# A mixer and mixture-of-experts layer on one core: row-tiled scatter, larger weight transfers, a reordered router and four experts written out

## What is computed

```
h      = rms_norm(x, norm_ffn_g)
logits = h @ w_router + b_router               # 256 x 32
top_v, top_e = top_k(logits, 4);  gate = softmax(top_v)
for each expert e, on the rows that chose it:
    gu = h @ w_gate_up[e] + b_gate_up[e]       # 1024 -> 2048
    g, lin = min(gu[:1024], 7), clip(gu[1024:], -7, 7)
    act = g * sigmoid(1.702 * g) * (lin + 1)
    y   = act @ w_down[e] + b_down[e]          # 1024 -> 1024
x = x + sum of gate * y over the four experts of a token
out = rms_norm(x, norm_final_g)
```

## Time and profile before

| | |
|---|---|
| median of 3 runs | 1145.58 us (1144.92 to 1145.92) |
| profiled execution | 1142.67 us, its span 1140.9 us |
| TensorE busy | 1113.5 us, 98% of the span |
| DVE, ACT, POOL busy | 24%, 16%, 7% |
| mean granted clock of TensorE | 0.988 |
| moved by transfers | 431.89 MB, 379 GB/s over the span |

### The profile page before, as it was taken

One profiled execution on the slowest core, in us unless ns is written; L12 is line 12 of the kernel. 1 busy time (PEld: TensorE's weight loads), 2 busy tenths in 40 slices (PEclk: granted clock), 3 DMA queues, 4 the chain that ended last, 5 costly groups with the idle time before them and its releaser, 6 DMA issues.

```text
span 1140.9 us, 12748 instructions
## 1 busy us (share of the span) xinstructions
PE 1113.5 (98%) x4959; PEld 490.8 (43%) x4960; DVE 273.7 (24%) x661; ACT 179.5 (16%) x333; POOL 75.9 (7%) x155
## 2 busy tenths in 40 slices
PE   7999899899999999999999999999999999999997
PEld 6888685533333333333333333333333333333332
DVE  3999761311111111111111111111111111111112
ACT  3011221111111111111111111111111111111112
POOL 2975100000000000000000000000000000000000
PEclk9999899799999999999999999999999999999999
DMA  8843479489999999999999999999999999999994
GB/s 225 268 157 139 159 304 374 185 327 410 418 418 428 430 427 429 429 427 430 427 429 429 429 429 429 427 430 427 428 429 427 430 427 428 429 429 429 429 427 191
DMA packets 51618, 431.89 MB, mean 379 GB/s; under 512 B 6465, under 2 KB 22255, under 8 KB 25390
## 3 DMA queue, kind: packets, MB, share of 16 engines
q1 hardware_dynamic: 51598, 431.62, 91.2%
HBM read 430.56 MB, written 1.05 MB: 378 GB/s over the span
## 4 chain that ended last, share of the span: by engine, by line
PE 89%; DVE 9%; issue 1%; ACT 1%; DMA 0%; DVEq 0%; another core or an unknown queue 0%; SPq 0%; POOL 0%; POOLq 0%
PE bank L1286 39%; PE bank L1298 20%; PE bank L1306 10%; DVE bank L814 6%; PE bank L1259 5%; PE bank L1265 3%; PE bank L1221 2%; PE bank L1186 2%; PE bank L1078 2%; PE bank L1278 1%; DVE bank L835 1%; PE bank L1270 1%; PE bank L1174 1%; PE bank L1252 1%; DVE ring L843 0%
## 5 line engine op out<-in xcount | busy, mean ns | idle before, releaser
L1286 PE MATMUL bank<-ring,area 128*64 128x512 f32 x2048 | 451.7, 593 | 0.8 <-DMA ring<-w_gate_up 0.8
L1286 PEld LDWEIGHTS bank<-ring,area 128*64 128x64 f32 x2048 | 147.4, 137 | 281.8 <-issue 273.5
L1298 PE MATMUL bank<-ring,area 128*64 128x512 f32 x1024 | 226.8, 595 | 1.0
L969 DVE TENSOR_SCALAR area<-bank 128x512 f32<-128x512 f32 x32 | 22.1, 692 | 769.8 <-PE bank L1286 769.8
L1298 PEld LDWEIGHTS bank<-ring,area 128*64 128x64 f32 x1024 | 70.7, 137 | 136.6 <-issue 127.9
L1306 PE MATMUL bank<-area,spT 128*128 128x512 f32 x256 | 118.4, 605 | 0.0
L1078 PE MATMUL bank<-area,ring 128*128 128x256 f32 x480 | 109.4, 388 | 1.2 <-DVE area L751 1.2
L1078 PEld LDWEIGHTS bank<-area,ring 128*128 128x128 f32 x480 | 92.5, 195 | 16.8 <-DMA ring<-w_in 1.4
L660 ACT ACTIVATE area<-area 128x512 f32<-128x512 f32 x32 | 20.2, 630 | 497.7 <-DVE area L969 497.7
L1306 PEld LDWEIGHTS bank<-area,spT 128*128 128x128 f32 x256 | 46.0, 189 | 71.9 <-issue 71.9
L814 DVE SCALAR_TENSOR_TENSOR bank<-ring,spread,bank 128x256 f32<-128x256 f32 x174 | 69.0, 481 | 0.0
(11 more groups left out here) (241 smaller groups left out, 522.8 us busy)
## 6 DMA issues: line engine op xcount, KB each, us to landing
ring<-w_gate_up SPq DMA_DIRECT2D x120, 2048.0 KB, 30.3
ring<-w_down SPq DMA_DIRECT2D x60, 2048.0 KB, 28.7
ring<-w_gate_up SPq DMA_DIRECT2D x16, 1024.0 KB, 12.0
ring<-w_in SPq DMA_DIRECT2D x15, 1024.0 KB, 9.6
ring<-w_down SPq DMA_DIRECT2D x8, 1024.0 KB, 13.2
ring<-w_out SPq DMA_DIRECT2D x1, 4096.0 KB, 14.0
ring<-w_conv_out SPq DMA_DIRECT2D x1, 3072.0 KB, 12.7
rows<-x SPq DMA_DIRECT2D x2, 512.0 KB, 3.8
```

Source lines behind the costliest of these rows:

```text
L969: return v.tensor_scalar(gc, bank[4][:, :], 7.0, None, ALU.min)
L1286: last = mm(bank[4 + b][64 * h:64 * h + 64, :], heT[:, k % 4, k // 4 * 64:k // 4 * 64 + 64], w[:, b * FF + h * 512:b * FF + h * 512 + 512] ...
L1298: last = mm(bank[6][64 * h:64 * h + 64, :], actT[:, k % 4, k // 4 * 64:k // 4 * 64 + 64], w[:, k % 2, h * 512:h * 512 + 512], start=(k == ...
```

## The change

- **Scatter.** `spT` loses its zero-padded halves: `scatter_half` uses only the 64 partitions that hold the rows, with 64 rows of the array; the four matmuls go to four banks and alternate between the array's row halves. `spread_copy` becomes one instruction. The memset of spT on POOL goes, and so does the memset of yrow on DVE, since the first expert has no scatter ahead of it.
- **Gather.** It moves from the middle of gate_up to behind the scatter.
- **Transfers.** A load may have 1, 2 or 4 slots. The refills after expert 0 to 3 are written out with the sizes in `EARLY`, those in the loop and after it are three of four slots (`MIDDLE`), and expert 31's are `LAST`, each with a semaphore of its own. TensorE waits for four slots at a time (`quad_in`), except in the last expert.
- **Router.** The rows are no longer multiplied by 1/rms but only by the norm's weights (`weighed_by_k`), with no wait for the variance; the factor 1/rms goes into the logits and into `pick`. b_router is added on DVE instead of by a ninth matmul. The gates of tile 0 are made before tile 1, those of tile 1 after the first picks. The four matmuls with b_down move behind gate_up of expert 0, and b_down lies elsewhere. The counts of `stay_warm` are 8, 2, 6, 3 instead of 4, 8 (two of the places are new).
- **Experts.** 0 to 3 and the last two are written out; the loop covers 4 to 29.

```diff
-WARM = 4, 8
+EARLY = (1, 1, 1, 1, 1, 1, 1, 1, 1, 1, 2), (2, 2, 2, 2, 2, 2), (2, 2, 2, 2, 4), (2, 2, 4, 4)
+MIDDLE = 4, 4, 4
+LAST = 4, 2, 2, 1, 1, 1, 1
+WARM = 8, 2, 6, 3
...
+            def refill(e, half, parts, signals=None):
...
+                j = 0
+                for p, n in enumerate(parts):
+                    sp.wait_ge(chunk_used, e * PER + j + n)
+                    load(e + 2, j, half, n, None if signals is None else signals[p])
+                    j += n
+            for e, parts in enumerate(EARLY):
+                refill(e, e % 2, parts)
+            with sp.Fori(len(EARLY) // 2, E // 2 - 2) as i:
                 for half in range(2):
-                    for j in range(0, PER, 2):
-                        sp.wait_ge(chunk_used, e * PER + j + 2)
-                        load_pair(e + 2, j, half)
+                    refill(i * 2 + half, half, MIDDLE)
+            refill(E - 4, 0, MIDDLE)
+            refill(E - 3, 1, LAST, end_in)
...
-                for h in range(2):
-                    last = s.activation(area[:, 512 * h + 1024 * t:512 * h + 1024 * t + 512], bank[2 * t + h][:, :], ACT.Square,
-                                        accum_out=ss4[:, 2 * t + h:2 * t + h + 1])
-                last.then_inc(x1_sq, 1)
+                for h in (1, 0):
+                    if h == 0:
+                        act.wait_ge(h_ready, 2 * t + 1)
+                    s.activation(area[:, 512 * h:512 * h + 512], bank[2 * t + h][:, :], ACT.Square,
+                                 accum_out=ss4[:, 2 * t + h:2 * t + h + 1]).then_inc(x1_sq, 1)
+                act.wait_ge(h2T_pe, 2 * t + 1)
+                s.activation(h2T[:, t, 0:4, :], grid(bank[4 + 2 * t][:, :], 4, 128), ACT.Copy).then_inc(h2T_act, 1)
                 act.wait_ge(var_h, t + 1)
                 s.activation(rstd[:, t:t + 1], ss[:, t:t + 1], ACT.Sqrt).then_inc(std_h, 1)
-                act.wait_ge(h2T_pe, 2 * t + 1)
-                s.activation(h2T[:, t, 0:4, :], grid(bank[4 + 2 * t][:, :], 4, 128), ACT.Copy).then_inc(h2T_act, 1)
-            for t in range(TT):
                 act.wait_ge(top8, t + 1)
                 s.activation(pe4[:, t, :], v8[:, t, 0:TOPK], ACT.Exp, bias=neg_top[:, t:t + 1],
                              accum_out=top_sum[:, t:t + 1]).then_inc(probs, 1)
...
+            def weighed_by_k(t):
+
                 dst = rows[:, t, :].rearrange("a (k p) -> a p k", p=128)
                 for h in range(2):
+                    if h == 1:
+                        dve.wait_ge(x1_sq, 2 * t + 1)
                     p, c = slice(h * 64, h * 64 + 64), slice(h * 512, h * 512 + 512)
-                    v.scalar_tensor_tensor(dst[:, p, :], grid(bank[2 * t + h][:, :], 64, KD), rstd[:, t:t + 1],
-                                           grid(gffn[:, c], 64, KD), ALU.mult, ALU.mult).then_inc(h_ready, 1)
+                    v.tensor_tensor(dst[:, p, :], grid(gffn[:, c], 64, KD), grid(bank[2 * t + h][:, :], 64, KD),
+                                    ALU.mult).then_inc(h_ready, 1)
...
+            def gates(t):
+
+                dve.wait_ge(probs, t + 1)
+                link(v.reciprocal(top_sum[:, t:t + 1], top_sum[:, t:t + 1]))
+                link(v.tensor_scalar(pe4[:, t, :], pe4[:, t, :], top_sum[:, t:t + 1], None, ALU.mult))
+                dve.wait_ge(mask_ready, t + 1)
+                link(v.tensor_tensor(selv[:, t], selv[:, t], pe4[:, t, :].unsqueeze(2).to_broadcast([128, TOPK, E]), ALU.mult))
+                v.tensor_reduce(gate[:, t, 0:E], selv[:, t].rearrange("p k e -> p e k"), AX.X, ALU.add).then_inc(gates_ready, 1)
...
-                link(v.tensor_copy(lg[:, t, :], bank[4 + 2 * t][:, 0:E]))
+                link(v.scalar_tensor_tensor(lg[:, t, :], bank[4 + 2 * t][:, 0:E], rstd[:, t:t + 1], brow, ALU.mult, ALU.add))
...
-                    v.tensor_scalar(pick[:, t, :], slot, rank[:, t, bass.ds(e, 1)], None, ALU.is_equal)
+                    v.tensor_scalar(pick[:, t, :], slot, rank[:, t, bass.ds(e, 1)], rstd[:, t:t + 1], ALU.is_equal, ALU.mult)
...
             picks(0, first, 0).then_inc(pick_ready, 1)
+            gates(1)
...
+            def scatter_half(n, stop=False):
+
+                r = slice(n % 2 * 64, n % 2 * 64 + 64)
+                return mm(bank[n][:, :], spT[r, n // 2, :], yrow[r, :], start=False, stop=stop, skip_group_check=True)
+
             def scatter():
                 for n in range(4):
-                    last = mm(bank[n][:, :], spT[:, n % 2, n // 2, :], yrow, start=False, stop=False, skip_group_check=True)
+                    last = scatter_half(n)
                 return last
...
+            def expert(e, half, uses):
+
+                gates_up(e, half, uses)
+                add_last(e)
+                fetch_next(e)
+                downs(e, half, uses)
+                more_blocks(e, half)
```

More of the change, by code:

```diff
@@ L14 @@
+import itertools
 import numpy as np
@@ L935, in _ @@
                 v.tensor_reduce(mask[:, t, :], selv[:, t].rearrange("p k e -> p e k"), AX.X, ALU.add).then_inc(mask_ready, 1)
[L937 to L941, removed]
-            dve.wait_ge(mask_ready, TT)
[L943 to L948, removed]
+                if t == 0:
+                    gates(0)
+            dve.wait_ge(mask_ready, TT)
             dve.wait_ge(cum_pe, 1)
@@ L1271, in spread_transposes, with arrived, gate_up @@
                 return last
-            def gate_up(half, buf, part=None, uses=None):
-                ks = range(KD) if part is None else range(4 * part, 4 * part + 4)
-                for b in range(2 if 0 in ks else 0):
+            def arrived(half, j, uses):
+                if uses is LAST:
+                    starts = [sum(LAST[:p]) for p in range(len(LAST))]
+                    if j in starts:
+                        pe.wait_ge(end_in[starts.index(j)], 16)
+                elif j % 4 == 0:
+                    pe.wait_ge(quad_in[half * 3 + j // 4], uses[j // 4])
+            def gate_up(half, buf, uses=None):
+                for b in range(2):
                     for h in range(2):
@@ L1279, in gate_up @@
                            start=True, stop=False)
-                for k in ks:
-                    if uses is not None and k % 2 == 0:
-                        pe.wait_ge(pair_in[(half * PER + k) // 2], uses)
+                for k in range(KD):
+                    if uses is not None:
+                        arrived(half, k, uses)
                     w = at(half * PER + k, CH)
@@ L1293, in down @@
                 for k in range(KD):
-                    if uses is not None and k % 4 == 0:
-                        pe.wait_ge(pair_in[(half * PER + KD + k // 2) // 2], uses)
+                    if uses is not None and k % 2 == 0:
+                        arrived(half, KD + k // 2, uses)
                     w = grid(at(half * PER + KD + k // 2, CH), 2, D)
@@ L1310, in _, with gates_up, fetch_next, downs @@
-            pe.wait_ge(down_in, 16)
-            down_bias(0)
-            down_bias(1)
+            def gates_up(e, half, uses, first=False):
+                pe.wait_ge(h_T, e + 1)
+                if not first:
+                    pe.wait_ge(spT_sb, e)
+                gate_up(half, half, uses)
+            def fetch_next(e):
+                pe.wait_ge(pick_ready, e + 2)
+                gather().then_inc(h_pe, 1)
+            def downs(e, half, uses):
+                pe.wait_ge(act_ready, e + 1)
+                transposes(gc, 4).then_inc(aT_pe, 1)
+                pe.wait_ge(h_row, e + 2)
+                transposes(hrow, 7).then_inc(hT_pe, 1)
+                pe.wait_ge(spread_ready, e + 1)
+                spread_transposes().then_inc(spT_pe, 1)
+                pe.wait_ge(a_T, e + 1)
+                down(half, uses)
@@ new lines, in add_last, with more_blocks @@
+            def add_last(e):
+                pe.wait_ge(y_row, e)
+                scatter()
+            def more_blocks(e, half):
+                with pe.If(any_more > 0):
+                    over = pe.value_load(nums[0:1, bass.ds(e, 1)], min_val=0, max_val=1)
+                    with pe.If(over > 0):
+                        before = pe.value_load(nums[0:1, bass.ds(e + E, 1)], min_val=0, max_val=E)
+                        pe.wait_ge(y_row, e + 1)
+                        pe.sem_inc(passed, 1)
+                        with pe.Fori(0, MORE) as b:
+                            o = before * MORE_STEPS + b * BLOCK_STEPS + 1
+                            pe.wait_ge(step, o)
+                            scatter().then_inc(step, 1)
+                            pe.wait_ge(step, o + 2)
+                            gather().then_inc(step, 1)
+                            pe.wait_ge(step, o + 4)
+                            transposes(hrow, 7)
+                            spread_transposes().then_inc(step, 1)
+                            pe.wait_ge(step, o + 6)
+                            gate_up(half, half).then_inc(step, 1)
+                            pe.wait_ge(step, o + 11)
```

(40 more changed lines are left out.)

155 lines of the change are left out of this document (52 added, 103 removed).

## The result

The changed kernel took 1130.31 us in the median of 4 runs (1130.06 to 1131.03) against 1145.25 us before: ratio 0.9879, 95% interval 0.9863 to 0.9896. A second set of runs on another chip gave 0.9890 (0.9867 to 0.9914). So it is 14.9 us faster; forecast were 18.6 less and 1127. The profiled execution took 1130.18 us, its span 1128.4 us (1140.9 before): between the two profiled executions it is 12.5 us.

A forecast was written before the change was run, and what follows sets the result against it. TensorE bound the chain, transfers 0.8 us behind. Refills starting 13.6 us earlier, stream latency and holes at 4 us, 2.6 saved by quads and an unchanged tail gave a span 18.4 less: 1145.6 - 18.4 = 1127 us, range 1118 to 1138.

The forecast's parts named there:

- The transfers as wall: Expert loop: transfers need 29.4 us per expert against TensorE's 26.4, so TensorE ends up waiting some 3 us per expert.
- The lead: Expert loop: the two experts of lead in the 24 slots, gone after about 14 experts at 3 us each.
- Start of the refills: Router, second token tile: first weights at 220.0 instead of 231.85, first refill at 222.3, 13.6 us earlier.
- a last part: End of the router's chain, from hrow's copy to the first gate_up weights: taken as 2.8 us, 216.7 to 219.5.
- the 0.5 us that were added for slow parts: Router: allowance for what still runs at a slow clock, moving the first weights from 219.5 to 220.0.
- TensorE's expert: Expert loop: TensorE's time per expert, 27.9 - 1.72 + 0.25 = 26.4 us, with the scatter at 1.9 us.
- Worth of the saving itself: nothing: Expert loop: TensorE's gain of 3 us per expert on the stream brings no time, as transfers set the end.
- the rival of the serial row halves: Scatter: row halves don't overlap, 28.55 us per expert, TensorE is the bound again, 1152 us; chance 0.05.
- DMAs of four slots: Refill stream: 0.06 us saved per DMA would make 5.2 us over 89 quads, or nothing; 2.6 taken.
- Latency and holes of the stream: From first refill to expert 31's last gate_up pair: 4 us beside 872.2 us at 428 GB/s; before, 6.2.
- The tail: From the landing of expert 31's last gate_up pair to the end of the span: 26.6 us, as before.
- Code: Written-out experts: TensorE stumbles, early four cost perhaps 1.2 us each, last two 3.35 each, 1138; chance 0.12 including half clock.

The follow-up runs named there:

- the fewer bytes: Changed kernel with each w_gate_up load from expert 2 on bringing only half the columns, 8.4 MB per expert instead of 12.6: 1082.54 us, ratio 0.9468.
- the old loop: Changed kernel with the expert stage as before (full-height scatter, gather inside gate_up, two-slot refills), new router kept: 1134.13 us, ratio 0.9928.
- the kernel with the moved code: Changed kernel with experts 30 and 31 waited for load by load, plus 46 matmuls in a never-taken branch ahead of TensorE's loop: 1127.32 us, ratio 0.9857.

## Why the prediction was right, point by point

- **The transfers as wall:** shown, by the chain after and by the fewer bytes (1082.5). The lead was to last about 14 experts: TensorE first waits for a load in expert 14, 0.23 us, and for 2.45 us in expert 15, at 631.87.
- **Start of the refills:** 220.01 and 222.17 us against 220.0 and 222.3 forecast. Each part of the router's chain came within 0.5 us. That the sum came out so exactly is partly luck: the gather ended 1.0 us late (217.66 for 216.7), and this was made good by a last part 0.5 us shorter than taken and by the 0.5 us that were added for slow parts.
- **TensorE's expert:** 26.54 us against 26.4; scatter 1.92 against 1.9. The Trainium skill (TensorEngine Tiling (Array Packing), Key Properties) has a change of mode drain the array; here the scatter takes 0.2 us over half of 3.43, the eight-fold of a full instruction's 0.43, and the gather 1.89 where it took 1.72 between matmuls of its own shape. The rows agree with the rule, and the price in them is 0.2 us a change.
- **"Worth of the saving itself: nothing":** right against the old loop (1133.7 with it, 1134.1 without), wrong as a margin. Put back alone, the full-height scatter makes 28.25 us per expert and 1139.7. That is the rival of the serial row halves, which the prediction priced at 28.55 and 1152; with 28.25 its own sum gives 1143 (1145.6 - 11.9 + 31 x 0.35 - 1.6). So the sum of the rival had the cost that this sentence left out. Between 27.9 and 28.25 TensorE becomes the bound over 32 experts, because two experts of lead must last for the whole loop. The row-tiled scatter is what lets the gather move.
- **DMAs of four slots:** 431 GB/s, the full 5 us of the bracket and not the half that I took.
- **Latency and holes of the stream, put at 4 us: the step that was mis-sized.** From 222.17 to the landing of expert 30's second quad at 1070.1 lie 344 slots, 360.7 MB, which at 431 GB/s take 836.9 of the 847.9 us: 11 us of latency and holes, 7 more than forecast. The faster rate gives 3.4 of them back: at 428 GB/s these slots would take 842.8 us, 5.9 more, and the forecast had 2.5 of that. Where the 11 us lie is known in part. Against 431 GB/s the stretches from 222 to 260 us lose 4.8: 1.6 in the first two, 1.6 between 240 and 250, the rest between. SP runs dry there: behind the eight loads up to 234.5 it issues the next at 243.13, since expert 0's down slots come free late and the next expert's after them. The four bias matmuls stand ahead of just these slots; that they are the cause was not tried. By 1070.1 the queue had moved 362.6 MB, 1.8 MB of it for later loads, and these are another 4.3 us.
- **The tail:** I had TensorE in step with the stream in expert 31. It ended gate_up 5.5 us later than forecast (1105.65 against 1100.1): 3.5 from the later landings, 1.7 from the hole at 1089.58. TensorE was what came last there: it waits for no load in expert 31, and in the kernel with the moved code, without the hole, it does.
- **Code:** the rival named it at 3.35 us for each written-out expert. It came twice, with 1.63 and 1.72 us. Through the first one the stream kept 429 GB/s (270 to 300 us), so only the last one counts.
- **Range:** both medians lie in 1118 to 1138. That the time is only 3.3 us over 1127 is in part luck. In spans the kernel gained 12.5 us where 18.4 were forecast, a miss of 5.9: the 5.5 us of the tail and 0.4 behind it. The forecast of the time had 2.9 us on top, by which the profiled execution of the kernel before lay under its median; the changed kernel's lies only 0.1 under its own, and that hides 2.8 of the 5.9.

## What to carry to other kernels

Where an engine and the transfers both look full, follow the time from issue to landing over the loop: if it grows, the transfers are the slower one, and the first load's start, the bytes and the rate set the end. Saving work on the engine pays only until its period falls below the point where the lead in the ring lasts to the end, and work put back can cost far more than the same work saved. What is left lies at the two ends of the stream: no hole behind the first refills, and loads waited for one by one in the last two experts, which the traces put at 0.4 to 1.6 us.

## What the runs showed of the hardware

- TensorE stood still for 0.5 to 6.1 us, with no releaser in the trace, at one or two places of most kernels. In those with written-out experts this was where it goes on with code that it has not run yet: ahead of experts 2 and 31 in the changed kernel (1.63 and 1.72 us, in its second trace 2.10 and 2.06), at the start of the loop with the code moved (6.06). In the kernel before it was the loop's first jump back, to code that it had run (2.50). Where depends on the code's position: with 19 matmuls fewer or 112 more in the router, and with 46 in a branch never taken, the hole ahead of expert 31 was gone. With the weight stream at 315 instead of 431 GB/s the same code had no hole at all. Code that is fetched behind queued weight loads would fit this; no run measured a fetch, and the cause stays open.
- A wait of 2.45 us in the middle of gate_up was followed by matmuls at a lower granted clock for a while (0.53 from 662 to 664 us; 8.81 instead of 6.87 us for 32), without cost where the transfers were the wall. In the last expert it costs: behind the hole of 2.06 us gate_up took 15.43 us for 13.74. It does not always come: behind 1.72 and 2.02 us at the same place the clock stayed at 1.00.
- Float32 matmuls on 64 of the array's rows, neighbours on different row halves and banks, overlapped: 1.92 us for eight instructions of 512 columns, against 3.63 at full height.
- Transfers of 4 MB moved 431 GB/s (changed kernel), of 2 MB 428 to 429 (kernel before, kernel with two-slot refills): some 0.06 us for each transfer.
